# Two output projections by seven block products in place of eight, with block sums on VectorE

## The reference

```
y = jnp.concatenate([ya, yb], axis=-1) @ w_out            # 1024 x 1024 weights
x = layer_norm(ALPHA * x + gate[:, None] * y, ln_g[l], ln_b[l])
```

## Time and profile before

| what | value |
|---|---|
| median of 3 runs | 1715.75 us |
| the profiled execution's own time | 1714.96 us |
| its span | 1713.2 us |
| TensorE busy | 1607.7 us, 94% |
| VectorE busy | 673.9 us, 39% |
| ScalarE busy | 549.4 us, 32% |
| mean granted TensorE clock | 0.987 |

### The profile page before, as it was taken

One profiled execution on the slowest core, in us unless ns is written; L12 is line 12 of the kernel. 1 busy time (PEld: TensorE's weight loads), 2 busy tenths in 40 slices (PEclk: granted clock), 3 DMA queues, 4 the chain that ended last, 5 costly groups with the idle time before them and its releaser, 6 DMA issues. The chain is left out here.

```text
span 1713.2 us, 26006 instructions
## 1 busy us (share of the span) xinstructions
PE 1607.7 (94%) x10106; PEld 1016.9 (59%) x10106; DVE 673.9 (39%) x1537; ACT 549.4 (32%) x1253; POOL 36.0 (2%) x108
## 2 busy tenths in 40 slices
PE   7999999899999998989999989999999889998996
PEld 4676866556555555555748656765564355555475
DVE  2123444414313214322346553235344255554166
ACT  0232142324323324432113332224214355554024
POOL 0000000000000000000000000000000011111000
PEclk9999999899999999999999999999999899999999
DMA  9100021122123013001634411000001000000344
GB/s 381 61 25 26 2 99 63 62 74 99 38 74 124 21 66 124 25 13 34 216 126 155 156 49 50 13 26 26 13 1 50 25 14 1 26 14 20 123 152 149
DMA packets 41145, 120.63 MB, mean 70 GB/s; under 512 B 4288, under 2 KB 14784, under 8 KB 39744
## 3 DMA queue, kind: packets, MB, share of 16 engines
q1 hardware_dynamic: 41024, 118.97, 19.8%
HBM read 109.52 MB, written 9.44 MB: 69 GB/s over the span
## 5 line engine op out<-in xcount | busy, mean ns | idle before, releaser
L1028 PE MATMUL proj<-hT,weights 128*128 128x512 f32 (+1 forms) x800 | 325.8, 553 | 7.5 <-DMA weights<-in_weights 2.8
L1028 PE MATMUL mixed<-hT,weights 128*128 128x512 f32 (+1 forms) x800 | 323.6, 550 | 2.5 <-DMA weights<-in_weights 1.3
L1028 PEld LDWEIGHTS proj<-hT,weights 128*128 128x128 f32 x800 | 147.0, 192 | 137.2 <-issue 128.8
L1028 PEld LDWEIGHTS mixed<-hT,weights 128*128 128x128 f32 x800 | 148.1, 193 | 128.6 <-issue 121.1
L1028 PE MATMUL mixed<-yT,weights 128*128 128x256 f32 (+1 forms) x432 | 123.0, 442 | 0.0
L1721 ACT ACTIVATE work<-turned 128x512 f32<-128x512 f32 (+2 forms) x136 | 72.7, 535 | 155.9 <-PE turned L1136 118.0
L1558 DVE SCALAR_TENSOR_TENSOR work<-work,turned 128x128 f32<-128x128 f32 (+1 forms) x152 | 53.1, 349 | 142.0 <-PE turned L1289 138.9
L1028 PEld LDWEIGHTS mixed<-yT,weights 128*128 128x128 f32 x432 | 82.1, 190 | 38.9 <-issue 31.1
L1028 PE MATMUL scores<-yT,weights 128*128 128x256 f32 (+1 forms) x320 | 91.3, 443 | 2.3 <-DVE yT L1487 2.3
L1721 ACT ACTIVATE work<-mixed 128x256 f32<-128x256 f32 (+1 forms) x85 | 32.7, 384 | 176.9 <-PE mixed L1190 170.2
L1721 ACT ACTIVATE work<-work,stat 128x640 f32<-128x640 f32 (+8 forms) x98 | 74.1, 757 | 22.1 <-DVE stat L1458 19.9
(11 more groups left out here) (267 smaller groups left out, 2203.6 us busy)
## 6 DMA issues: line engine op xcount, KB each, us to landing
weights<-in_weights SPq DMA_DIRECT2D x138, 512.0 KB, 3.7
tables<-in_bias SPq DMA_DIRECT2D x8, 1281.0 KB, 8.3
hT<-in_xT SPq DMA_DIRECT2D x8, 640.0 KB, 16.0
yT<-in_weights SPq DMA_DIRECT2D x8, 512.0 KB, 8.4
work<-in_xT SPq DMA_DIRECT2D x24, 128.0 KB, 3.4
x1T<-yT SPq DMA_DIRECT2D x12, 256.0 KB, 2.2
work<-in_weights SPq DMA_DIRECT2D x4, 512.0 KB, 17.0
pair<-in_weights SPq DMA_DIRECT2D x4, 512.0 KB, 17.8
```

The lines of the kernel that those rows point to most:

```text
L1028: last = nc.tensor.matmul(PJ[BANK_OF[u]][:, 0:n], weights[:, w % WBUFS, k, :], src[:, k, t0:t0 + n], start=(k == 0), stop=(k == KT - 1))
```

## The change

Both output projections, except for the last 256 tokens, are computed in blocks of two by two: a pair of output tiles (`g`), two halves of the 8 feature tiles that are summed over, and two halves of the tokens. Seven products of blocks (`m` 1, 6, 5, 7, 2, 3, 4, in that order; each is 4 float32 products) stand where eight stood. They need sums of weight blocks (`wsum`, four operations on 512 columns for each pair, in tiles loaded once more from memory by `load_raw` and used by both passes) and sums of token blocks (`tsum`, four operations on 4 x n columns for each pass). There are two passes in each layer: in layer 0 n is 256 and the passes cover tokens 0 to 1023, in layer 1 n is 192 and they cover tokens 256 to 1023. ScalarE copies the first and the fifth product out of their banks, onto which products 2 and 3 are then added; VectorE combines the partial results. The last 256 tokens go as before. The chunks of the norms, the assumed lengths that `pace` uses, and the order of layer 1's first projections change with it.

```diff
-NORMS = [(0, CTX), (CTX, 512), (CTX + 512, 256), (CTX + 768, 256)]
+LAST = CTX + 768
+FAST = (((0, 256), (512, 256)), ((CTX, 192), (CTX + 384, 192)))
+NORMS = ([(0, 256), (256, 256), (512, 512), (LAST, 256)], [(0, 0), (CTX, 384), (CTX + 384, 384), (LAST, 256)])
...
+def paced(l, ci, head, centre, square, scale, following=0.8):
+    us = {"centre": centre, "square_sum": 0.0, "rstd": 1.6, "scale": scale, "next": following}
+    out = [(None, head), (("column_sum", l, ci), 1.1)]
+    for x in norm(l, ci):
+        out += [(None, square)] * (x[0] == "square_sum") + [(x, us[x[0]])]
+    return out
...
+def fast_projection(l, ps):
+    out = []
+    for g in range(KT // 2):
+        first, middle, second, third = (Slot() for _ in range(4))
+        out += [("fast", l, ps, g, m, u) for m, u in ((1, first), (6, middle), (5, second), (7, third), (2, first),
+                                                      (3, second), (4, third))]
+    return out
...
+def with_sums(products, sums):
+    out = []
+    for s in products:
+        out.append(s)
+        if s[0] == "fast" and s[4] == 4:
+            out += [x for g, x in sums if g == s[3]]
...
-    s += sum(gates[18:], [])
-    s += [("banks", 6)] + out_projection(0, 0, NORMS[:1])
-    parts = [out_projection(0, ci, NORMS[ci:ci + 1]) for ci in range(1, 4)]
-    s += [("blend",)] + pace(normalise(0, 0), parts[0])
+    s += gates[18] + [("wsum", 0, 0)] + gates[19] + [("wsum", 0, 1)] + gates[21] + gates[22] + [("tsum", 0, 0)]
+    s += gates[20] + gates[23] + [("banks", 6)]
+    s += with_sums(fast_projection(0, 0), [(0, ("wsum", 0, 2)), (1, ("wsum", 0, 3)), (2, ("tsum", 0, 1))])
+    s += [("blend",)] + pace(paced(0, 0, 4.0, 1.4, 2.9, 0.8) + paced(0, 1, 0.0, 1.4, 2.9, 0.8), fast_projection(0, 1))
...
-    ready = [gates[0][0], gates[1][0]] + q[:4] + [gates[0][1], gates[1][1]] + k[:8] + v[:12]
-    rest = [gates[2][0], q[4], gates[2][1]] + q[5:] + [("rows", 1)] + k[8:] + v[12:] + [("rows_exp",)]
-    s += pace(middle_norms(), parts[1] + parts[2] + ready) + [("rows", 0)] + rest
+    ready = [gates[0][0]] + k[:4] + [gates[0][1]] + v[:8]
+    ready += [gates[1][0]] + q[:4] + [gates[1][1]] + k[4:8] + v[8:16]
+    rest = [gates[2][0], q[4], gates[2][1]] + q[5:] + [("rows", 1)] + k[8:] + v[16:] + [("rows_exp",)]
+    s += pace(paced(0, 2, 3.0, 1.5, 2.9, 0.8, 0.7) + paced(0, 3, 0.0, 0.9, 2.0, 0.6, 0.6),
+              out_projection(0) + ready) + [("rows", 0)] + rest
...
-    s += attention(1, [rq[1], rq[2], rq[3], gates[7]], gates[4:7])
-    s += [("banks", 6)] + out_projection(1, 1, NORMS[1:2])
-    parts = [out_projection(1, ci, NORMS[ci:ci + 1]) for ci in range(2, 4)]
-    s += pace(last_norms(), parts[0] + parts[1])
+    last = attention(1, [rq[1], rq[2], rq[3], gates[7]], gates[4:7])
+    for i, x in ((4, ("tsum", 1, 0)), (5, ("wsum", 1, 0))):
+        last.insert([s[:2] for s in last].index(("pv", ("att", 1, 3, i))) + 1, x)
+    s += last + [("banks", 6)]
+    s += with_sums(fast_projection(1, 0), [(0, ("tsum", 1, 1)), (0, ("wsum", 1, 1)), (1, ("wsum", 1, 2)),
+                                           (2, ("wsum", 1, 3))])
+    s += pace(paced(1, 1, 3.5, 1.7, 2.5, 1.2), fast_projection(1, 1))
+    s += pace(paced(1, 2, 2.5, 1.2, 3.0, 0.75), out_projection(1))
...
+                if s[0] == "scores" and s[1] == ("att", 0, 3, 4):
+                    sp.wait_ge(*at(("att_pe", 0, 2)))
+                    load_raw(0, range(4))
+                if s[0] == "mm" and s[1] == ("gate", 0, 6) and s[7] == 0 and s[3] == 0:
+                    sp.wait_ge(*at(("att_pe", 0, 3)))
+                    load_raw(0, range(4, 8))
+                if s[0] == "scores" and s[1] == ("att", 1, 1, 0):
+                    sp.wait_ge(*at(("lin_pe", True, 1)))
+                    sp.wait_ge(*at(("lin_dve", True, 1)))
+                    load_raw(1, range(7))
+                if s[0] == "scores" and s[1] == ("att", 1, 3, 4):
+                    sp.wait_ge(*at(("att_pe", 1, 2)))
+                    load_raw(1, range(7, 8))
...
+            def s_fast(l, ps, g, m, u):
+                t0, n = FAST[l][ps]
+                one, two = (WEIGHT_AT[("out", l, 2 * g + x, ps)] for x in range(2))
+                if m in (1, 6, 5, 7):
+                    wait_bank(pe, u)
+                if m == 1:
+                    pe.wait_ge(*at(("tsum", l, ps)))
+                    pe.wait_ge(*at(("weight", one)))
+                    left, right = weights[:, one % WBUFS, 0:4, :], yT[:, 0:4, t0:t0 + n]
+                elif m == 2:
+                    pe.wait_ge(*at(("first_kept", l, ps, g)))
+                    left, right = weights[:, one % WBUFS, 4:8, :], yT[:, 4:8, t0:t0 + n]
+                elif m == 4:
+                    pe.wait_ge(*at(("weight", two)))
+                    pe.wait_ge(*at(("seventh_read", l, ps, g)))
+                    left, right = weights[:, two % WBUFS, 4:8, :], token_sum(l, ps, 4)
+                else:
+                    if m == 6:
+                        pe.wait_ge(*at(("wsum", l, g)))
+                    if m == 3:
+                        pe.wait_ge(*at(("fifth_kept", l, ps, g)))
+                    left = weight_sum(l, g, m)
+                    right = yT[:, 4:8, t0 + n:t0 + 2 * n] if m == 3 else token_sum(l, ps, m)
+                for k in range(4):
+                    last = nc.tensor.matmul(PJ[BANK_OF[u]][:, 0:n], left[:, k, :], right[:, k, :],
+                                            start=(k == 0 and m in (1, 6, 5, 7)), stop=(k == 3), skip_group_check=True)
+                done(last, ("fast", l, ps, g, m),
+                     *([("weight_used", one)] if m == 2 else [("weight_used", two)] if m == 4 else []))
...
+            def s_wsum(l, g):
+                dve.wait_ge(*at(("raw", l, g)))
+                (a11, a12), (a21, a22) = ([x[:, 0:512], x[:, 512:D]] for x in (raw_tile(l, 2 * g), raw_tile(l, 2 * g + 1)))
+                link(V.tensor_tensor(a22, a21, a22, ALU.add))
+                link(V.tensor_tensor(a21, a11, a21, ALU.subtract))
+                link(V.tensor_tensor(a11, a22, a11, ALU.subtract))
+                link(V.tensor_tensor(a12, a12, a11, ALU.subtract), ("wsum", l, g))
+            def s_tsum(l, ps):
+                t0, n = FAST[l][ps]
+                if l == 0:
+                    dve.wait_ge(*at(("att_pe", 0, 3)))
+                b11, b12, b21, b22 = (yT[:, k:k + 4, t:t + n] for k in (0, 4) for t in (t0, t0 + n))
+                t1, t2, t4 = (token_sum(l, ps, m) for m in (5, 6, 4))
+                link(V.tensor_tensor(t1, b12, b11, ALU.subtract))
+                link(V.tensor_tensor(t2, b22, t1, ALU.subtract))
+                link(V.tensor_tensor(b12, b22, b12, ALU.subtract))
+                link(V.tensor_tensor(t4, b21, t2, ALU.subtract), ("tsum", l, ps))
...
+            def s_fast(l, ps, g, m, u):
+                t0, n = FAST[l][ps]
+                f1, f2 = 2 * g, 2 * g + 1
+                ps_ = PJ[BANK_OF[u]][:, 0:n]
+                r1, r2 = (RESID_AT[(l, f, t0)] for f in (f1, f2))
+                first, second = (x_stage[r1 % 4][:, x:x + n] for x in (0, n)), (x_stage[r2 % 4][:, x:x + n] for x in (0, n))
+                (res11, res12), (res21, res22) = first, second
+                kept, fifth, u2, u3 = (partial(x, n) for x in range(4))
+                def gate(f, half):
+                    w = 1 if half == 0 and t0 == 0 else 0
+                    return mods[:, l, 16 + f, w:w + 1]
+                def add(out, in0, f, half, res, *keys):
+                    link(V.scalar_tensor_tensor(out=out, in0=in0, scalar=gate(f, half), in1=res, op0=ALU.mult,
+                                                op1=ALU.add), *keys)
+                def total_of(f):
+                    link(V.tensor_tensor(total(t0, 2 * n), hT[:, 0, t0:t0 + 2 * n] if f == 1 else total(t0, 2 * n),
+                                         hT[:, f, t0:t0 + 2 * n], ALU.add),
+                         *([("total", l, f, lo) for lo, w in NORMS[l] if w and t0 <= lo < t0 + 2 * n] if f == KT - 1 else []))
+                if m != 1 and m != 5:
+                    dve.wait_ge(*at(("fast", l, ps, g, m)))
+                if m == 6:
+                    dve.wait_ge(*at(("first_kept", l, ps, g)))
+                    link(V.tensor_tensor(u2, ps_, kept, ALU.add), ("proj_free", u), ("first_used", l, ps, g))
+                elif m == 5:
+                    dve.wait_ge(*at(("resid", r1)))
+                    dve.wait_ge(*at(("resid", r2)))
+                    add(res12, u2, f1, 1, res12)
+                    add(res21, u2, f2, 0, res21)
+                elif m == 7:
+                    link(V.tensor_tensor(u3, ps_, u2, ALU.add), ("seventh_read", l, ps, g))
+                    dve.wait_ge(*at(("fifth_kept", l, ps, g)))
+                    link(V.tensor_tensor(u3, u3, fifth, ALU.add), ("fifth_used", l, ps, g))
+                    add(hT[:, f2, t0 + n:t0 + 2 * n], u3, f2, 1, res22)
+                elif m == 2:
```

(36 more changed lines are left out.)

106 lines of the change are left out of this document (68 added, 38 removed).

## The result

The change made the kernel 0.66% slower: 1727.43 us median of 5 runs (1722.18 to 1727.98) against 1713.96 (1712.29 to 1716.87), ratio 1.0066, 95% interval 1.0046 to 1.0087. The forecast was 1712.5 in a range of 1701 to 1722. The profiled execution took 1727.79 us, with a span of 1726.0.

A forecast was written before the change was run, and what follows sets the result against it. TensorE's work plus its waits was taken as the time. Layer 0's -16.8 us and layer 1's +13.8 us sum to -3.0 on the profiled 1714.96, 1712.0; the median forecast was 1712.5, case range 1706 to 1718, overall range 1701 to 1722.

The forecast's parts named there:

- the price of the clock behind a wait: Time lost to a lowered TensorE clock after new waits: 1.5 us in layer 0 and 5.1 us in layer 1.
- the cover of the gate rows: Layer 0: value products moved ahead bring TensorE to `h1` at 138 us, ready at 121; no gate-row wait was priced.
- Products: Output projections: fewer TensorE products save 13.8 us in layer 0 and 8.9 in layer 1, at 0.1645 us per 192-column record.
- Rival (d): Layer 1: weight loads are not covered at 192 columns, 0.190 us a record, +11.4 us, 1724; chance 0.03.
- VectorE's prices: Cost of VectorE's added steps: `wsum` 2.9 us, `tsum` 5.0 in layer 0 and 3.9 in layer 1.
- the waits of layer 1: TensorE waits 6.8, 2.85 and 2.85 us for pair sums in the first pass, and 4.1 us at square sums.
- Layer 0: Its stretch: -13.8 us of products, -12.5 of old waits and clock, +9.5 of new ones; -16.8 us, ends -22 and -10.
- The waits at the square sums: Layer 0, second pass: TensorE waits 8.0 us for VectorE's norms, about 1.2, 2.9 and 3.9 at three `square_sum`.
- End of the attention: Layer 1's first sums delay reciprocals by 2.3 and about 5.0 us; its first pass starts 2.6 us later, bounds 0 and 4.5.
- Layer 1's clock: Clock lost behind layer 1's new waits: 2.6 us for the longest plus 3 x 0.85, 5.1 us.
- (b): Rival: each of six waits in layers 0 and 1 costs 2.6 us of half clock, 15.6 us, 1721.5; chance 0.17.
- the prediction's own walk: Stepping along VectorE's order in the second passes to find when TensorE waits: 8.0 us in layer 0, 4.1 in layer 1.

The follow-up runs named there:

- the run with the rows' order: Both new placements of layer 1's sums, plus layer 0's four moved value products put back behind the gate rows; 1697.33 us, ratio 0.9901 to the kernel before.
- The run of the attention's end: The change with layer 1's first sums put singly into VectorE's gaps of the attention, none ahead of a reciprocal; 1719.36 us, ratio 1.0018 to the kernel before.

## Why the prediction was wrong, point by point

The direction of each changed stretch was right, the sum was not: -3.0 us forecast, +12.8 measured on the profiled executions. The main failing step is the price of the clock behind a wait: 6.6 us in the sum, 14.7 measured (below), 8.1 of the 15.8 us that were missed. The second is the cover of the gate rows, taken to cost nothing: 2.9 us. Another 4.6 us fell outside the changed stretches. Layer 1's output products began 1.7 us earlier than before, where 14 was said.

- **Products: right.** 448 records of 256 columns in layer 0 at 0.216; 192 columns at 0.1625 a record (1.30 for eight) against the 0.1645 chosen. Rival (d) is out, though its 1724 was the number nearest to 1727.4.
- **VectorE's prices and the waits of layer 1: right.** 6.8, 2.9 and 2.9 us on line 1098 against 6.8, 2.85, 2.85; 3.9 us at the square sums against 4.1; line 1179 no longer waits on `hT`, and no wait on a weight tile stands in the lists above.
- **Layer 0: -16.8 forecast, -12.9 measured.** The waits at the square sums are 7.4 us against 8.0. Their half clock is 3.1 against 1.5: 1.7 behind the third, and 1.4 behind the second, where the lines below take 5.36 us, up to the next instruction at 925.49, in place of 3.98; the prediction had counted that one as made good by a shorter third wait. And the gate rows: the prediction counted the values of tokens up to 1023, moved ahead, as cover for `h1`, and did not ask what they had covered where they stood. It was the rows' chain on VectorE and ScalarE, and taking them away opened 2.9 us, which the run with the rows' order gave back with 1 us more.

```profile
920.13 1.22 PE L1168 MATMUL turned<-kvV,consts 128*128 128x256 f32 x2 [3.40 <-DVE kvV L1860]
921.14 4.51 PE L1148 MATMUL mixed<-yT,weights 128*128 128x256 f32 x16
```

- **End of the attention: +2.6 forecast, +6.6 measured.** The first reciprocal was late by 4.1 us (3.9 said), the second by 7.7 (5.0 said), as half clock stands ahead of it; the transposes waited 2.3 and 3.1 us. The prediction priced only the length and put the clock at nothing, without a reason. Behind both waits the products ran at half clock: 1.7 + 0.4 + 1.7 us, 3.8. The run of the attention's end took back 8.1, the two waits and most of the clock.
- **Layer 1's clock: +5.1 forecast, 7.8 measured**: 2.4 + 1.8 + 1.8 behind the sums, 1.8 behind the first square sum. The prediction took short waits at half of one observed loss, because one wait of 2.3 us in the trace had been free. The same wait (2.34 us, the same 32 records of 512 columns behind it) stands in the two kernels with seven products in layer 0 alone: in one profile they take 15.67 us, in the other 13.97, as before.
- **Outside the change: 0 forecast, +2.1 and +2.5 measured**, with the same instructions. 1.7 of it is one stretch of 16 records behind an unchanged wait of 2.1 us, before and after (the two lines below). In the stretch from the gate rows to the attention's end TensorE is busy 1.6 us longer for the same work and idles 0.9 us more.

```profile
758.75 3.68 PE L1028 MATMUL proj<-hT,weights 128*128 128x256 f32 x16
```

```profile
758.95 5.37 PE L1148 MATMUL proj<-hT,weights 128*128 128x256 f32 x16
```

Of the 14 profiles of this study 8 have half clock in that stretch and 6 have not.

The rival whose mechanism came nearest is (b), 1721.5: six waits with a stretch of half clock each, 15.6 us. The changed stretches have nine waits over 2 us, and behind them 14.7 us are lost: 1.4, 1.7 and 0 in layer 0 (the last is the gate rows' wait), 2.1 and 1.7 at the attention's end, 2.4, 1.8, 1.8 and 1.8 in layer 1. Its total was near, for smaller losses at more waits; what it lacked is the rows' wait and the clock outside the change.

The prediction took its price from three waits of the trace, which had cost 1.7, 2.6 and nothing, and charged it to fewer waits than it forecast. The same trace has four more waits over 2 us outside the changed stretches. One, of 2.10 us, cost nothing; the others, of 2.02, 2.08 and 3.67 us at 1198, 1324 and 1337 us, cost 1.7, 1.7 and 3.3. All seven make 1.6 us on average. With the eight waits over 2 us that follow from the prediction's own walk (two in layer 0, two at the attention's end, four in layer 1) that is 12.6 in place of 6.6 and a forecast of 1718.5: no longer faster. With the rows' wait, length and clock, it is 1723. The rest of the way to 1727.4 lies outside the change.

## What to carry to other kernels

A product saved is worth its spacing only if the sums that replace it are made where nobody waits for them: the same instructions, one at a time in the gaps of the engine that makes them, turned +13.5 us into -13 and, with the gate rows' wait closed and the square sums later, -21. Price every wait of TensorE over 2 us at its length and the mean clock loss of all such waits in the trace, free ones counted, and do so in every stretch, not only where the wait is longest. When work is moved ahead as cover for one chain, ask what it covered where it stood; and when a step is moved on all engines' lists at once, an engine that is behind stays behind.
